# A mixture-of-experts stage on TensorE: 64-token groups in two column strips against 32-token groups in four, with the down product dealt into the next group

## The reference, cut to what matters

```python
logits = tok @ w_router + b_router                   # 256 x 32
top_val, top_idx = lax.top_k(logits, 4); top_w = softmax(top_val)
# for the tokens of expert e:
hgu  = tok[rows] @ w_gu[e] + b_gu[e]                 # 1024 -> 2048
gate = minimum(hgu[:, 0::2], 7.0)
up   = clip(hgu[:, 1::2], -7.0, 7.0)
act  = (up + 1.0) * (gate * sigmoid(1.702 * gate))   # 1024 wide
y    = act @ w_down[e] + b_down[e]                   # 1024 -> 1024
out[rows] += y * wts
```

## Time and profile before

| | |
|---|---|
| median of 3 runs | 1385.5 us (1385.05 to 1386.11) |
| span of the profiled execution | 1383.6 us |
| TensorE busy (PE) | 1307.4 us, 94% |
| weight loads (PEld), VectorE, ScalarE | 44%, 20%, 18% |
| DMA | 455.91 MB, mean 330 GB/s |
| mean granted TensorE clock | 0.986 of full |

### The profile page before, as it was taken

One profiled execution on the slowest core, in us unless ns is written; L12 is line 12 of the kernel. 1 busy time (PEld: TensorE's weight loads), 2 busy tenths in 40 slices (PEclk: granted clock), 3 DMA queues, 4 the chain that ended last, 5 costly groups with the idle time before them and its releaser, 6 DMA issues.

```text
span 1383.6 us, 15858 instructions
## 1 busy us (share of the span) xinstructions
PE 1307.4 (94%) x6029; PEld 613.6 (44%) x6030; DVE 281.6 (20%) x831; ACT 250.2 (18%) x514; POOL 18.5 (1%) x26
## 2 busy tenths in 40 slices
PE   8999999999889999999999999999999999999998
PEld 4664858886443333333343333333333333333332
DVE  3234333651410111101111112011110110111011
ACT  2124421460111111110111101111011110111101
POOL 1100000000000000000000000000000000000000
PEclk9999999999889999999999999999999999999999
DMA  9942355223687999986938999999999999999991
GB/s 335 316 151 73 111 196 197 94 81 122 257 356 319 427 427 426 427 340 265 425 160 369 425 427 427 427 426 423 426 426 428 426 425 425 425 427 427 426 423 69
DMA packets 66261, 455.91 MB, mean 330 GB/s; under 512 B 7284, under 2 KB 13016, under 8 KB 33432
## 3 DMA queue, kind: packets, MB, share of 16 engines
q1 hardware_dynamic: 65528, 454.13, 79.8%
q0 software_dynamic: 256, 0.79, 0.2%
q10 hardware_dynamic: 448, 0.60, 0.1%
HBM read 454.45 MB, written 1.05 MB: 329 GB/s over the span
## 4 chain that ended last, share of the span: by engine, by line
PE 78%; DMA 17%; ACT 2%; DVE 1%; issue 1%; ACTq 0%; SPq 0%; DVEq 0%
PE bank L1007 25%; DMA ring<-in_w_down 17%; PE bank L1037 15%; PE bank L555 6%; PE bank L695 6%; PE bank L978 4%; PE bank L994 3%; PE bank L970 3%; PE bank L604 2%; PE bank L891 2%; PE bank L857 2%; PE bank L544 1%; PE bank L1026 1%; ACT mq L1303 1%; PE bank L581 1%
## 5 line engine op out<-in xcount | busy, mean ns | idle before, releaser
L1007 PE MATMUL bank<-ring,sp_ 128*64 128x512 f32 x2176 | 479.9, 599 | 0.0
L1007 PEld LDWEIGHTS bank<-ring,sp_ 128*64 128x64 f32 x2176 | 154.4, 138 | 324.0 <-issue 324.0
L1037 PE MATMUL bank<-ring,mq 128*64 128x512 f32 x1088 | 245.7, 601 | 35.6 <-ACT mq L1303 23.7
L1037 PEld LDWEIGHTS bank<-ring,mq 128*64 128x64 f32 x1088 | 76.7, 138 | 181.3 <-issue 153.7
L1735 DVE TENSOR_SCALAR sp_<-bank 128x256 f32<-128x256 f32 x68 | 28.5, 420 | 572.2 <-PE bank L1007 572.2
L1299 ACT ACTIVATE sp_<-sp_ 128x256 f32<-128x256 f32 x68 | 28.3, 416 | 509.2 <-DVE sp_ L1735 509.2
L555 PE MATMUL bank<-ring 128*128 128x512 f32 x192 | 83.2, 592 | 0.0
L1751 DVE TENSOR_SCALAR sp_<-cst,rank_it,w_it 128x64 f32<-128x64 f32 x68 | 16.7, 311 | 280.2 <-PE bank L1007 280.2
L695 PE MATMUL bank<-ring 128*128 128x256 f32 x320 | 71.3, 381 | 0.0
L970 PEld LDWEIGHTS bank<-sp_,sc 128*128 128x128 f32 x544 | 64.5, 198 | 15.2 <-issue 15.2
L994 PE MATMUL bank<-bg,cst 1*64 1x512 f32 x272 | 66.9, 609 | 3.8 <-issue 3.8
(11 more groups left out here) (293 smaller groups left out, 839.9 us busy)
## 6 DMA issues: line engine op xcount, KB each, us to landing
ring<-in_w_gu SPq DMA_DIRECT2D x128, 2048.0 KB, 25.1
ring<-in_w_down SPq DMA_DIRECT2D x64, 2048.0 KB, 16.5
ring<-in_w_in SPq DMA_DIRECT2D x13, 2048.0 KB, 10.4
ring<-in_w_out SPq DMA_DIRECT2D x2, 2048.0 KB, 8.5
ring<-in_w_mem_kv SPq DMA_DIRECT2D x2, 1024.0 KB, 7.4
ring<-in_w_mem_kv SPq DMA_DIRECT2D x1, 2048.0 KB, 8.0
ring<-in_cmp_w_k SPq DMA_DIRECT2D x1, 2048.0 KB, 8.5
ring<-in_cmp_w_v SPq DMA_DIRECT2D x1, 2048.0 KB, 8.5
```

Source lines behind the costliest of these rows:

```text
L1007: mm = nc.tensor.matmul(BH[b][64 * hh:64 * hh + 64, :], xgT[:, k, 64 * par:64 * par + 64], w[:, c, o:o + 512], start=False, stop=k == KT - ...
L1037: mm = nc.tensor.matmul(BG[64 * hh:64 * hh + 64, :], actT[:, o:o + 64], w[:, c, 512 * hh:512 * hh + 512], start=k == 0, stop=k == KT - 1, ...
```

## The change

`SLOT_TOK` becomes 32, so the same counts make 45 groups, 46 with the empty one, 23 pairs: experts 1, 6, 8, 12, 15, 19, 22 and 24 have two groups, expert 7 three, expert 9 four. The gate/up and down products of a group go to four 32-column strips of the array instead of two of 64 (for down, even and odd rows of the activation go to different strips, and the scatter adds them, `Gw` having each slot twice). The down product of a group no longer follows its own gate/up product: its transposes come behind quarter 0 and the bias of the next group, and its product behind quarter 1. The two activations have buffers of their own (`actT[par]`, `gt`, `ut`, `sg`, and one bank of `BH` each). The first pair and the last are written out, the dummy scatter of the first pair and its two fills are gone, the product with `b_dn` comes ahead of the last pair, and round 1 of the loads takes the steady order. The tables grow by 7 columns, the list of groups from 48 to 64 entries, and the scratch of the DMA queues is set to 4096 bytes.

In the diff, removed lines stand only where they are short; the functions that they belong to are printed above.

```diff
-SLOT_TOK = 64
+SLOT_TOK = 32
...
-            load_round(1, True, [0, 1, 2, 3, 4, 5])
             steady = [0, 1, 4, 5, 2, 3]
+            load_round(1, True, steady)
...
-                for half, b in ((1, BX), (0, BG)):
+                for half, b in ((0, BX), (1, BG)):
                     for c in range(4):
-                        for i in range(NT):
+                        for t in range(NT):
                             o = P * (4 * half + c)
-                            mm = nc.tensor.matmul(b[:, P * c:P * c + P], x2[:, i, o:o + P], Gm[:, i, :],
-                                                  start=i == 0, stop=i == NT - 1)
+                            mm = nc.tensor.matmul(b[:, 64 * c:64 * c + 64], x2[:, t, o:o + P], Gm[:, t, :],
+                                                  start=t == 0, stop=t == NT - 1)
                     mm.then_inc(S("g_full"), 1)
 
...
+            def bias(par, row):
+                p = 32 + 32 * row
+                for s in range(4):
+                    mm = nc.tensor.matmul(BH[par][32 * s:32 * s + 32, :], ones[p:p + 1, 0:32], brow[row][:, 512 * s:512 * s + 512],
+                                          start=False, stop=False, skip_group_check=True)
+                mm.then_inc(S("brow_used"), 1)
+            def up(q, e, par, row):
+                slot = q + NSLOT if row else q
+                if q == 0:
                     pe.wait_ge(brow_in[row], e * 8 + (8 if row else 16))
+                pe.wait_ge(w_full[slot], e * 8 + (8 if row else 16 * (TRUNK_TURNS + 1)))
+                w = ring[:, slot, :].rearrange("p (c n) -> p c n", c=2)
+                for c in range(2):
+                    k = 2 * q + c
+                    for s in range(4):
+                        mm = nc.tensor.matmul(BH[par][32 * s:32 * s + 32, :], xgT[:, k, 32 * par:32 * par + 32],
+                                              w[:, c, 512 * s:512 * s + 512], start=k == 0, stop=k == KT - 1,
+                                              skip_group_check=True)
+                mm.then_inc(S("gu_done"), 1)
+            def turn(i, par, pairs=None):
+                pe.wait_ge(S("act_ready"), i + 1)
+                for two in range(2):
+                    a = ut[par].rearrange("p (f two) -> p f two", two=2)[:, :, two]
+                    mm = nc.tensor.transpose(BX[:, P * two:P * two + P], a, ident)
+                if par:
+                    pe.wait_ge(S("Gw_ready"), pairs)
+                    for t in range(NT):
+                        mm = nc.tensor.transpose(BX[:, 256 + P * t:256 + P * t + P], Gw[:, t, :], ident)
                 mm.then_inc(S("a_full"), 1)
+            def down(i, e, par):
                 pe.wait_ge(S("a_evac"), i + 1)
                 for d in range(2):
                     pe.wait_ge(w_full[4 + d], e * 16 + 16 * (TRUNK_TURNS + 1))
                     w = ring[:, 4 + d, :].rearrange("p (c n) -> p c n", c=4)
+                    for c in range(2):
+                        for two in range(2):
+                            o = P * two + 32 * (2 * d + c)
+                            for hh in range(2):
+                                mm = nc.tensor.matmul(BG[64 * hh + 32 * two:64 * hh + 32 * two + 32, :], actT[par][:, o:o + 32],
+                                                      w[:, 2 * c + two, 512 * hh:512 * hh + 512],
+                                                      start=d + c == 0, stop=d + c == 2, skip_group_check=True)
                     mm.then_inc(S("down_done"), 1)
+            def item(at, most):
+                return pe.value_load(idx[0:1, at], min_val=0, max_val=most)
+            def either(odd, work):
+                with pe.If(odd > 0):
+                    work(1)
+                with pe.Else():
+                    work(0)
+            def pair(j, first=False, final=False):
+                i0, i1 = j * 2, j * 2 + 1
+                e0, e1 = [item(bass.ds(j * 2 + (NE + par), 1), NE - 1) for par in range(2)]
+                odd0, odd1 = [item(bass.ds(j * 2 + (NE + ITEMS + par), 1), 1) for par in range(2)]
+                if not first:
+                    before_e = item(bass.ds(j * 2 + (NE - 1), 1), NE - 1)
+                def left(row):
+                    pe.wait_ge(S("g_evac"), j * 2 + 1)
+                    up(0, e0, 0, row)
+                    bias(0, row)
+                    if not first:
+                        turn(j * 2 - 1, 1, j)
+                    up(1, e0, 0, row)
+                    pe.wait_ge(S("g_evac"), j * 2 + 2)
+                    if not first:
+                        down(j * 2 - 1, before_e, 1)
+                    up(2, e0, 0, row)
+                    up(3, e0, 0, row)
+                def right(row):
+                    up(0, e1, 1, row)
+                    bias(1, row)
+                    if not final:
+                        turn(i0, 0)
+                    up(1, e1, 1, row)
+                    if not final:
+                        down(i0, e0, 0)
+                    up(2, e1, 1, row)
+                    up(3, e1, 1, row)
+                either(odd0, left)
+                if not first:
+                    pe.wait_ge(S("y_evac"), j * 2)
+                    pe.wait_ge(S("st_evac"), j)
+                    scatter()
+                either(odd1, right)
                 if not final:
                     pe.wait_ge(S("G_ready"), j + 2)
+                    pe.wait_ge(S("y_evac"), j * 2 + 1)
                     gather()
...
+            pair(0, first=True)
+            with pe.Fori(1, last_pair) as j:
                 pair(j)
+            pe.wait_ge(S("bdn_in"), 16)
+            for i in range(NT):
+                for hh in range(2):
+                    nc.tensor.matmul(ACC[i][hh][:, :], rTs[:, 256 + P * i:256 + P * i + P],
+                                     b_dn[:, 512 * hh:512 * hh + 512], start=False, stop=False, skip_group_check=True)
             pair(last_pair, final=True)
+            e0, e1 = [item(bass.ds(last_pair * 2 + (NE + par), 1), NE - 1) for par in range(2)]
+            turn(last_pair * 2, 0)
+            down(last_pair * 2, e0, 0)
+            turn(last_pair * 2 + 1, 1, last_pair + 1)
+            pe.wait_ge(S("y_evac"), last_pair * 2 + 1)
+            down(last_pair * 2 + 1, e1, 1)
...
+            def gates(i, par):
+                act.wait_ge(S("g_clip"), i + 1)
+                nc.scalar.activation(sg[par], gt[par], ACT.Sigmoid, scale=ALPHA).then_inc(S("g_sig"), 1)
+            def results(i, par, scattered=None):
+                nc.scalar.activation(actT[par], BX[:, 0:256], ACT.Copy).then_inc(S("a_evac"), 1)
+                if scattered is not None:
+                    act.wait_ge(S("scattered"), scattered)
+                if par:
+                    nc.scalar.activation(STs, BX[:, 256:512], ACT.Copy).then_inc(S("st_evac"), 1)
...
+            results(last_pair * 2 - 1, 1)
+            gates(last_pair * 2, 0)
+            gates(last_pair * 2 + 1, 1)
+            results(last_pair * 2, 0, last_pair)
+            results(last_pair * 2 + 1, 1)
...
```

More of the change, by code:

```diff
@@ L162, in const_table @@
     add("sinc", s)
-    add("iota", np.tile(np.arange(SLOT_TOK, dtype=np.float32), (P, 2)))
+    add("iota", np.tile(np.arange(ITEMS, dtype=np.float32), (P, 1)))
+    add("slots", np.tile(np.arange(SLOT_TOK, dtype=np.float32), (P, 2)))
+    add("full", np.tile(np.arange(SLOT_TOK, SEQ, SLOT_TOK, dtype=np.float32), (P, 1)))
     add("sum4", np.tile(np.eye(32, dtype=np.float32), (4, 1)))
@@ L339, in hybrid_layer @@
         Eit = bg1[0:32, 1312:1312 + ITEMS]
[L340 to L344, removed]
+        Ait = bg1[0:32, 1376:1376 + ITEMS]
+        count = bg1[0:32, 1306:1307]
+        cntc = bg1[0:32, 1440:1440 + SEQ // SLOT_TOK - 1]
+        few = bg1[0:1, 1448:1448 + ITEMS // 2 - 1]
+        nlast = bg1[0:1, 1480:1481]
+        before = bg1[0:1, 1488:1488 + NE]
         ACC = [[banks[2 * i + h] for h in range(2)] for i in range(NT)]
@@ L1021, in down @@
-            def down(i, e):
-                pe.wait_ge(S("act_ready"), i * 2 + 2)
-                for q in range(4):
-                    a = act_sb[:, 256 * (q // 2):256 * (q // 2) + 256].rearrange("p (f two) -> p f two", two=2)[:, :, q % 2]
-                    mm = nc.tensor.transpose(BX[:, P * q:P * q + P], a, ident)
+            def bias(par, row):
[4 more added lines that the diff above has]
+                mm.then_inc(S("brow_used"), 1)
@@ L1040, in down @@
-                    mm.then_inc(S("down_done"), 1)
-            def pair(j, final=False):
-                e0, e1 = [pe.value_load(idx[0:1, bass.ds(j * 2 + (NE + par), 1)], min_val=0, max_val=NE - 1)
-                          for par in range(2)]
-                odd0, odd1 = [pe.value_load(idx[0:1, bass.ds(j * 2 + (NE + ITEMS + par), 1)], min_val=0, max_val=1)
-                              for par in range(2)]
-                pe.wait_ge(S("g_evac"), j * 2 + 2)
-                pe.wait_ge(S("st_evac"), j + 1)
-                up(j * 2, e0, odd0, 0)
```

(24 more changed lines are left out.)

153 lines of the change are left out of this document (52 added, 101 removed).

## The result

The change makes the kernel 3.3% slower: 1430.4 us median of 4 runs (1429.9 to 1433.0) against 1385.6, a ratio of 1.0331 [1.0315, 1.0348]. The forecast was 1386.7, in a range of 1376 to 1399: wrong by 43.7 us. The profiled execution has a span of 1428.3 us; its mean granted clock fell from 0.986 to 0.917. In the kernel after, line 1005 is the gate/up product (1007 before), 1032 the down product (1037), 991 the bias (994), 972 the gather (970), 980 the scatter (978), 1015 and 1019 the transposes, 1038 the load of a register, 1096 the loop over pairs, and 365 the issue of weights (363).

A forecast was written before the change was run, and what follows sets the result against it. Weights pace one-group experts, TensorE two-group ones; expert 10's down release sets the last landing (1358.4). The work behind it ends at 1380.3; 4.5 for the clock and 1.9 from span to median give 1386.7, range 1376 to 1399.

The forecast's parts named there:

- The group's size and the four strips: TensorE's work per 32-token group: four strips halve gate/up, bias and down, so a group takes 15.7 us, against 28.4 before.
- Rival E: Four strips on TensorE give less than twice two; at a rate halfway, a group takes 21.4 and the kernel 1456; chance 0.05.
- rival F: TensorE's time halves everywhere and the load queue never pauses: 61 us off the last landing, about 1323; chance 0.03.
- Expert 7's start: Start of the heavy stretch on TensorE, after waits for weights: 580.3, where it was 590.7 before.
- 9 x 15.7 = 141.3: Heavy stretch, experts 7 to 9: nine groups take 141.3 us, against 142.0 for five before; down of expert 10 released at 728.3.
- rival D: Sequencer's loads, loop and branch at pair ends are not hidden: 2 to 8 us in the stretch, 1389 to 1395; chance 0.08.
- the margin is 2.0 us: Later two-group experts (12, 15, 19, 22, 24): next down chunk lands after 22.9, needed at 24.9, so the queue does not pause.
- the 4.5 that the forecast had for the clock: Lower clock after waits: 1.2 at expert 7's start, 1.2 at the end, 5 x 0.3 at margins, 0.6 inside the stretch.
- Rival C: The clock falls inside the heavy stretch, where bias, transposes and gather leave the array partly empty: 1394.6; chance 0.24.
- the same: Whole kernel: gains and losses cancel, no change beyond 0.2%, 1382.7 to 1388.3; chance 0.30.
- The 10.4 us of the earlier start are eaten by 9.9 of later release: Expert 7 starts 10.4 earlier, but expert 10's down chunk is released 6.7 behind the last group's end, formerly 3.2 ahead.
- The empty group: End of the kernel: the empty 46th group is computed like any other, 7.9 for gate/up and bias plus 3.5 for down.

The follow-up runs named there:

- e1: The changed kernel with TensorE's register loads spread over a pair, only two left at its start: 1393.5 us, ratio 1.0058.
- e9: The changed kernel with three unused full-array matmuls of 512 columns behind every gather: 1416.3 us, ratio 1.0224.
- e5: The changed kernel with register loads spread over a pair and no work for the empty 46th group: 1378.3 us, ratio 0.9961.
- e6: As e5, with the dealt down product brought forward, behind quarter 0 of the next group and ahead of its bias: 1375.2 us, ratio 0.9929.
- e3: The changed kernel without dealing: groups of 32 in four strips, each down product behind its own group's gate/up product: 1412.6 us, ratio 1.0201.
- e4: The kernel before with four more, unused, register loads at the top of every pair: 1446.2 us, ratio 1.0440.

## Why the prediction was wrong

**The group's size and the four strips: right.** Gate/up takes 1.92 a quarter as a row shows it (1.74 by the next start), 109 ns a record against 217. Rival E (four strips less than twice two) and rival F fall. A change of shape costs little: a quarter takes 1.86 to the start of the bias (582.54 to 584.40) and 1.74 to that of a down product of its own shape. The pair from 712.30 to 746.55 is 34.25, of which 2.6 is idle: 15.8 a group against 15.7. The Trainium skill (TensorE: Matmul & The Clock Gate, Part 3) has three column tiles at 2.38 times one. Here four strips, at 109 ns a record of 512 columns, gave twice what two gave, so the trace does not bear out a loss of that kind.

**Expert 7's start and the count of groups: near.** It starts at 582.5 for 580.3, and there are 46 groups.

**The step that failed is the pair's end**, which the sum had at nothing: "9 x 15.7 = 141.3" has no term for it. The cause stood in the text as rival D, "five register loads, a loop and a branch, with half the queued work to hide them", but at 2 to 8 us, 1389 to 1395, and a chance of 0.08. It took 0.44 to 1.67 for each pair end from two places that are unlike this one. Two readings of the trace of before would have sized it: the loop's instruction at 728.28 beside the bias at 732.65, and the steps of 0.77. A branch and loop of 0.8 as above (4.66 less five steps of 0.77) and five steps are 4.66; half of 4.37 is 2.2; the idle is 2.5.

And each end counted three times over. From the release at 757.06 instead of 728.3, 28.8 us late: the start 2.2; five pair ends 2.52, 2.66, 2.52, 2.50 and 2.61, 12.8; half clock behind them 1.6, 4.1 and 3.2 in three of the groups, 8.9, and none behind the end at 712.30; 3.8 in the group that holds the release, 3.2 of it by half clock; 1.1 left over. Then the two-group experts: "the margin is 2.0 us, so no pause, as long as the clock is full". A pair end of 2.5 overruns it, and 764.4 + 622.7 = 1387.1 became 1403.2, 16.1 of pauses (0.4 in e1). The tail adds 3.2. 28.8 + 16.1 + 3.2 is 48.1; less the 4.5 that the forecast had for the clock, 43.6, against 1428.3 − 1384.8 = 43.5.

**The clock: a fall behind idle was right, its place and size off.** Rival C had it fall between shapes. The forecast gave 0.6 for falls inside the stretch. e1 and e9 show that alternating shapes leave it at 1.00 there; it fell behind idle, and e9 puts a floor of 14 us under its cost.

**With the loads spread, the forecast's sum nearly holds.** e1 has 1393.5 for 1386.7, inside the whole range but above the 1388.3 at which "the same" ended: expert 7 starts at 584.7, 4.4 later than "580.3" (behind two waits for weights of 3.77 and 1.85, with halves of the down product at 3.13 and 3.64 instead of 1.92), nine groups take 3.0 more, so the release at 735.7 is 7.4 late, the last landing 8.0, and the tail of 25.2 is 3.3 longer: 8.0 + 3.3 − 4.5 = 6.8, which is 1391.6 − 1384.8. The 4.5 set aside for the clock thus covered part of what the other terms lacked, which is luck. "The 10.4 us of the earlier start are eaten by 9.9 of later release" was near for the second number; of the first, 6.0 came. The five margins held.

**The empty group.** The forecast would be wrong if it delayed the end by more than 8 us; it does: it costs 13.8 of tail (25.1 against 11.3), of which the forecast had 7.9 for its gate/up and bias and 3.5 for its down product. Nearly all of it was in the forecast's 21.9, so it did not make the error; it hid what the change could gain, as e5 and e6 show.

How the 23 us from e9 to e1 divide is seen: the release moves by 13.9, the pauses shrink from 10.8 to 0.4. What stays open is why a fall of the clock costs 1.6 us behind one pair end, 3 to 4 behind others and nothing behind the one at 712.30.

## What to carry to other kernels

Before work is made smaller, look at what the engine's sequencer does between two pieces of it: the lead at which it runs ahead shrank with the length of the queued matmuls (4.37 us at 217 ns each, 2.15 and 2.7 at 114 and 108), so shorter matmuls leave less time to hide loads, loops and branches. Read the lead off the trace (the loop's instruction against the end of the work ahead of it), count the loads at 0.77 each, and spread them over the pair when they don't fit. When a margin elsewhere is of the size of the new gap (2.0 here), price both: of 45 us, 16 came from overrun margins.

## What was unexpected of the hardware

The sequencer's lead was 4.37 us ahead of a down product in two strips, 2.15 ahead of the gather in the kernel after, and 2.7 ahead of a down product in four strips (e3): about 20, 19 and 25 matmul records, and as many weight loads. The Trainium skill (TensorE: Matmul & The Clock Gate, Architectural detail) gives TensorE's queue a depth of 64; by it the lead in the kernel after would have been, as an estimate, 32 pairs of weight load and matmul, 3.6 us. All three traces show fewer.

A register load in TensorE's sequencer took 0.30 us, 0.77 with the operations behind it. The Trainium skill (DMA: Bandwidth & Descriptors, Latency and other measured facts) has a floor of about 600 ns for a `tensor_load`, without saying where from. The trace has half of that for the load from SBUF and more for the whole step.

The clock fell behind a short idle in work that was otherwise dense. TensorE had been busy from 582.54 to 598.33 without a gap; behind the idle of 2.52 the granted clock was 0.52 over 3.5 us. In the kernel before with more loads, e4 shows the same behind 2.03. Behind 0.56 (e9) and behind 1.16 (e3) the next quarter took 1.92 and 1.93, at full clock. But the length of the idle does not decide it alone: behind 2.50 at 712.30 the quarter took 1.92, and in e3, where a down product and not the gather stands ahead of the idle, so it did behind 2.07, 2.03 and 2.06 (at 881.95, 1032.63 and 1305.54). The slowed quarter is likely, and not certain, behind such an idle.
